# Square sums of latents, keys and channels: added over chunks on GpSimd and VectorE, then one TensorE product with a block of ones that sums and spreads

## The chip, the cores and the metric

One core of one Trainium2 chip runs the whole program. The metric is the device time in microseconds of one execution. The kernel is written directly on the engines: TensorE (PE), VectorE (DVE), ScalarE (ACT), GpSimd (POOL) and SyncE (SP) each have their own instruction list, and only semaphores order them against each other.

## The reference

Two transformer-like blocks of two layers each are run over 256 tokens (T) with a model width of 2048. The parts that matter are three norms inside each layer of the first block:

- Latents: z @ w_in gives a query latent of 512 and a key/value latent of 256 features. Each is divided per token by its root mean square, sqrt(mean(z²) + 1e-6), and multiplied by a gain.
- Keys: each of four heads has a key of 192 features, 128 of its own and 64 rotated ones that all heads share. Each is divided per token by the root mean square over the 192.
- Channels: the 512 channels of a causal 31-tap convolution go through a layer norm, so they need a mean and a mean of squares per token.

Everything is float32.

## The kernel before

Activations lie with features on the 128 partitions and tokens along the free axis, in chunks of 128 features; a tile of four chunks is 128 x 4 x 256. A norm therefore has to sum over partitions, which TensorE does by a product with ones, and the per-token result has to come back to every partition.

**Streams.** Weights come as slabs of 128 x 2048 float32 (1 MB), one DMA each on SyncE's queue into a ring of four (`raw`). ScalarE copies a slab to a rounded high part (`whi`, L1164, 1.92 us), VectorE subtracts to get the low part (`wlo`, L1630, 2.29 us), three slabs ahead of TensorE. TensorE multiplies each slab by the high and low parts of the activations H: 16 products of 512 columns (L642) and 16 of 256 (L653), about 5.5 us a slab. VectorE then takes the bank out and scales it (L1651, L1661).

**Order.** The first block's layer is a list of numbered slabs, by hand: zq 0 to 5, zkr 6, cfg 7 to 10, cfa 11 to 14, kv 15, qn 16, qr 17, ret 18 to 25, sc 26 to 37, rg 38 to 41, then wo. Each engine walks through the same numbers. For slab s it does its stream work and then the side work tied to s: TensorE in `within_first` (inside the slab) and `behind_first` (behind it), ScalarE in `beside_first`, VectorE in `before_first` and `after_first` (before and after its split). Side work on an engine stands in its program order, so whatever it waits for holds up the slab work behind it.

**The three norms before.** All three use the columns trick. The squares are the stationary operand and a single column of ones is streamed, which gives a sum per token on partitions (128 tokens at a time); ScalarE takes a root over a few columns, VectorE inverts them (`invert`, L1679), and `spread` (L767) brings them back by a product of the broadcast column with the identity.

- Latents: ScalarE squares into w4 and z[12:14] at slab 5; `lora_sums` (L758) runs within slab 7 and behind slab 7, 6 products of one column each time; root at 8 (L1280), invert at 8, spread of 4 behind 9, `lora_scaled` (L1782) at 9; `lora_low` at 11 hands the result to kv at slab 15.
- Keys: the rotated key is squared at 9 and the keys at 15 (ScalarE, L1266); `key_sums` (L776, L779) is called behind 16, between the units qn and qr, 10 products; then four transposes (L879); root (L1299) and `invert` at 16; `spread` of 8 behind 18; `keys_scaled` (L1812, L1816) at 18 reads the spread from PSUM. `query_turned` (L1825 to L1827) follows at 19, and `scores` (L840) behind slab 20 wait for it.
- Channels: VectorE computes the 31 taps of chunks 24 and 25 of z (L1774), GpSimd those of 26 and 27 (L529) out of products that ScalarE makes (L1381). `channel_sums` (L807) behind 36 adds the four chunks by four products with ones; VectorE centres them at 36 (L1902), ScalarE squares at 37 (L1266), `channel_squares` (L815) behind 38 takes 8 one-column products; root at 38 (L1324), invert, `spread` of 2 behind 39, scaling at 39 (L1909).

Each float32 product stands as two instructions in the trace (a count of x8 is four products). GpSimd is idle during slabs 0 to 12 and after its last tap (slab 28) until wo. Lengths that matter: `rstd` is 128 x 512, `tmp` 128 x 4 x 256, `sqacc` and `sqtmp` 128 x 256.

```python
def rooted(n=T, o=0):
    dve.wait_ge(S("root"), nth("root"))
    link(dve.reciprocal(rstd[:, o:o + n], rstd[:, o:o + n]))
def invert(columns):
    dve.wait_ge(S("root"), nth("root"))
    dve.reciprocal(inv_rms[:, 0:columns], inv_rms[:, 0:columns]).then_inc(S("inverted"), 1)
```

Of the kernel before, what the change touches and what calls it, by code (L numbers as in the profile page):

```python
# [27 lines left out]
P = 128  # L28
# [227 lines left out]
def _build(nc, d, out, ctx):  # L256
# [205 lines left out]
    def _(pool):  # L462
# [54 lines left out]
        for l in range(L):  # L517


            for c in POOL_CF:  # L520
# [3 lines left out]
                for s in range(1, 31):  # L524
# [6 lines left out]
                    done["tap"] += 1  # L531
            square_sum(slab_of(("wo", l)))
# [30 lines left out]
    def _(pe):  # L563
# [189 lines left out]
        def lora_sums(l, t):  # L753

            pe.wait_ge(S("lora_sq"), l + 1)
            for first, count, src in ((0, 4, w4[:, 0:4, :]), (2, 2, z[:, 12:14, :])):
                for c in range(count):
                    last = pe.matmul(pX[:, first + t:first + t + 1], src[:, c, t * P:(t + 1) * P], ones[:, 0:1],  # L758
                                     start=c == 0, stop=c == count - 1, skip_group_check=True)
            if t:  # L760
                last.then_inc(S("lora_sums"), 1)

        def spread(places):

            pe.wait_ge(S("inverted"), nth("spread"))
            for dst, c in places:
                last = pe.matmul(dst, inv_rms[:, c:c + 1].to_broadcast([P, P]), C("ident"),  # L767
                                 start=True, stop=True, skip_group_check=True)
            last.then_inc(S("spread"), 1)

        def key_sums(l):

            pe.wait_ge(S("key_sq"), l + 1)
            for t in range(2):
                tok = slice(t * P, (t + 1) * P)
                pe.matmul(pX[:, 4 * t:4 * t + 4], z[:, 6, tok], C("halves", 0, 1).to_broadcast([P, 4]), start=True,  # L776
                          stop=False, skip_group_check=True)
                for h in range(HEADS):
                    last = pe.matmul(pX[:, 4 * t + h:4 * t + h + 1], w4[:, h, tok], ones[:, 0:1], start=False,  # L779
                                     stop=True, skip_group_check=True)  # L780
            last.then_inc(S("key_sums"), 1)
# [20 lines left out]
        def channel_sums(l):  # L802

            pe.wait_ge(S("cf_taps"), 31 * len(DVE_CF) * (l + 1))
            pe.wait_ge(S("cf_pool"), 30 * len(POOL_CF) * (l + 1))
            for c in range(4):
                last = pe.matmul(pX[:, 0:T], ones[:], z[:, 24 + c, :], start=c == 0, stop=c == 3)  # L807
            last.then_inc(S("cf_sum"), 1)

        def channel_squares(l):  # L810

            pe.wait_ge(S("cf_sq"), l + 1)
            for t in range(2):
                for c in range(4):
                    last = pe.matmul(pX[:, t:t + 1], z[:, 16 + c, t * P:(t + 1) * P], ones[:, 0:1], start=c == 0,  # L815
                                     stop=c == 3, skip_group_check=True)
            last.then_inc(S("cf_sums"), 1)
# [147 lines left out]
        def within_first(l, s):  # L965

            if s == 7:
                if l == 0:
                    pe.wait_ge(S("const_in"), 16)
                lora_sums(l, 0)  # L970
# [10 lines left out]
        def behind_first(l, s):  # L981
# [10 lines left out]
            if s == 13:  # L992
                pe.wait_ge(S("turn_gains"), l + 1)
                pe.wait_ge(S("evac"), by["zkr", l].first + 1)
                turn_halves(vtok[:, 0:P], [small[:]], pO)
# [6 lines left out]
            if s == 18:  # L1002
                spread([((pX, pX, pO, pO)[h][:, (h % 2) * T + t * P:(h % 2) * T + (t + 1) * P], 4 * t + h)
# [1279 lines left out]
```

## Time and profile before

| what | value |
|---|---|
| device time, median of 3 runs | 3350.71 us (3349.78 to 3351.73) |
| the profiled execution's own time | 3352.41 us |
| its span, first to last instruction | 3350.2 us |
| mean granted TensorE clock | 0.998 |
| TensorE busy | 3327.6 us, 99% |
| VectorE, ScalarE, GpSimd busy | 78%, 46%, 26% |

Times in the views are microseconds from the span's start. A line such as `start length engine line operation out<-in shape xcount` merges neighbouring instructions of one kind; a bracket behind it is idle time of that engine before it and what ended it. A product's duration includes its way through the array, so products overlap: what a group costs TensorE is read from its start to the start of what comes next. Layer 0 of the first block runs its slabs 0 to 41 from about 11 to 284, layer 1 from about 1209 to 1475.

### The profile page before, as it was taken

The numbers are of one execution on the slowest core, as the hardware profiler recorded it, in microseconds if no ns is written. First come the engines' busy times: TensorE is split into PE (matmuls) and PEld (weight loads), VectorE is DVE, ScalarE is ACT, GpSimd is POOL, SyncE is SP. The second block draws the span as 40 slices with busy tenths as digits, with TensorE's granted clock in tenths as the row PEclk, the third lists the DMA queues.
The fourth block names the chain that finished last, engine by engine and source line by source line (L and its number), as shares of the span: only waits on it lengthen the run. The fifth ranks groups of instructions, "written<-read, shape, count | busy, mean of one in ns | idle before, by whom it ended". The sixth has DMA issues, their size and how long they took to land. (4 is left out here: it accounts for less than half of the span.)

```text
span 3350.2 us, 53769 instructions
## 1 busy us (share of the span) xinstructions
PE 3327.6 (99%) x20366; PEld 2929.1 (87%) x20366; DVE 2617.8 (78%) x3394; ACT 1531.6 (46%) x1642; POOL 864.2 (26%) x633
## 2 busy tenths in 40 slices
PE   9999999999999999999999999999999999999998
PEld 8989888888888989888888888888888888888897
DVE  8897788787786888887887787867867866678865
ACT  5644444343433556544443434335444444445443
POOL 0422432121122423414332121214432004150004
PEclk9999999999999999999999999999999999999999
DMA  6445555555555554455555555555544455544454
GB/s 241 148 163 176 189 188 189 178 202 177 206 174 189 203 182 165 151 176 187 190 188 178 198 180 199 180 190 200 193 164 153 167 173 189 180 164 151 167 185 151
DMA packets 90647, 605.21 MB, mean 181 GB/s; under 512 B 10192, under 2 KB 10352, under 8 KB 29296
## 3 DMA queue, kind: packets, MB, share of 16 engines
q1 hardware_dynamic: 89424, 599.83, 52.0%
q10 hardware_dynamic: 1056, 3.11, 0.2%
q8 instruction: 110, 1.80, 0.2%
q14 instruction: 57, 0.47, 0.0%
HBM read 600.80 MB, written 2.10 MB: 180 GB/s over the span
## 5 line engine op out<-in xcount | busy, mean ns | idle before, releaser
L642 PE MATMUL bank<-H,whi 128*128 128x512 f32 x6496 | 1574.3, 393 | 1.5 <-DVE z L1661 1.5
L1164 ACT ACTIVATE whi<-raw 128x2048 fp32r<-128x2048 f32 (+2 forms) x609 | 1093.6, 1796 | 1044.6 <-DMA raw<-in_slabs_down 259.8
L1630 DVE TENSOR_TENSOR wlo<-raw,whi 128x2048 fp32r<-128x2048 f32 (+2 forms) x609 | 1328.4, 2181 | 243.2 <-ACT whi L1164 233.1
L642 PEld LDWEIGHTS bank<-H,whi 128*128 128x128 f32 x6496 | 1188.7, 188 | 238.6 <-issue 5.9
L653 PEld LDWEIGHTS bank<-H,wlo 128*128 128x128 f32 x6624 | 849.1, 188 | 34.3
L653 PE MATMUL bank<-H,wlo 128*128 128x256 f32 x6624 | 871.1, 281 | 0.0
L511 POOL TENSOR_TENSOR sqtmp<-tmp 128x256 f32<-128x256 f32 x88 | 218.9, 2488 | 867.8 <-DVE tmp L2211 867.8
L642 PE MATMUL bank<-G,whi 128*128 128x512 f32 x1408 | 343.0, 391 | 0.0
L642 PEld LDWEIGHTS bank<-G,whi 128*128 128x128 f32 x1408 | 255.4, 188 | 48.0
L1564 ACT ACTIVATE G<-sqtmp 128x256 f32 (+1 forms) x88 | 36.8, 418 | 404.0 <-POOL sqtmp L511 404.0
L489 POOL TENSOR_TENSOR sqacc<-sqacc,sqtmp 128x256 f32<-128x256 f32 x119 | 199.4, 1676 | 9.4
L1651 DVE TENSOR_REDUCE tmp<-bank 128x256 f32<-128x512 f32 x216 | 149.0, 690 | 65.9 <-PE bank L653 65.4
L484 POOL TENSOR_TENSOR sqtmp<-x 128x256 f32<-128x256 f32 x119 | 133.7, 1123 | 238.5 <-DVE x L1705 182.5
L653 PEld LDWEIGHTS bank<-G,wlo 128*128 128x128 f32 x1408 | 184.3, 189 | 9.8
L529 POOL TENSOR_TENSOR z<-z,y 128x255 f32<-128x255 f32 (+14 forms) x120 | 121.1, 1009 | 269.9 <-ACT y L1381 254.2
L1704 DVE TENSOR_TENSOR x<-x,bank 128x256 f32 (+1 forms) x192 | 80.7, 420 | 138.8 <-PE bank L653 138.7
L653 PE MATMUL bank<-G,wlo 128*128 128x256 f32 x1408 | 186.8, 281 | 0.0
L1651 DVE TENSOR_REDUCE z<-bank 128x256 f32<-128x512 f32 x132 | 91.0, 690 | 103.1 <-PE bank L653 102.0
L484 POOL TENSOR_TENSOR sqacc<-x 128x256 f32<-128x256 f32 x8 | 16.3, 2031 | 589.0 <-DVE x L1705 547.1
L676 PE MATMUL bank<-whi,H 128*128 128x512 f32 x320 | 129.9, 406 | 0.0
L678 PE MATMUL bank<-whi,H 128*128 128x512 f32 x320 | 126.1, 394 | 0.0
L677 PE MATMUL bank<-wlo,H 128*128 128x512 f32 x320 | 126.0, 394 | 0.0
(390 smaller groups left out, 2881.4 us busy)
## 6 DMA issues: line engine op xcount, KB each, us to landing
raw<-in_slabs_up SPq DMA_DIRECT2D x176, 1024.0 KB, 4.8
raw<-in_slabs_down SPq DMA_DIRECT2D x128, 704.0 KB, 4.0
raw<-in_slabs_wo SPq DMA_DIRECT2D x32, 1024.0 KB, 4.8
raw<-in_slabs_pg SPq DMA_DIRECT2D x32, 1024.0 KB, 4.9
raw<-in_slabs_gates SPq DMA_DIRECT2D x32, 1024.0 KB, 4.9
raw<-in_slabs_wout SPq DMA_DIRECT2D x32, 1024.0 KB, 4.8
raw<-in_slabs_sc SPq DMA_DIRECT2D x24, 1024.0 KB, 4.8
raw<-in_slabs_fox SPq DMA_DIRECT2D x24, 1024.0 KB, 4.9
```

The source lines that it names most:

```text
L484: pool.tensor_tensor((sqtmp if c else sqacc)[:], x[:, c, :], x[:, c, :], ALU.mult).then_inc(S("pool_sq"), 1)
L489: ins = pool.tensor_tensor(sqacc[:], sqacc[:], sqtmp[:], ALU.add)
L511: pool.tensor_tensor(act_f[:], tmp[:, 3, :], tmp[:, 2, :], ALU.mult).then_inc(S("act_f32"), 1)
L529: pool.tensor_tensor(o[:, s:T], o[:, s:T], product[:, done["tap"] % TAP_RING, s:T], ALU.add).then_inc(S("cf_pool"), 1)
L642: pe.matmul(b[0:r.m, :], whi[:, n % RAW, w], r.src[:, k, :], start=at == 0, stop=False)
L653: last = pe.matmul(b[0:r.m, 0:T], wlo[:, n % RAW, w], r.src[:, k, 0:T], start=False, stop=at == r.kt - 1)
L676: pe.matmul(b[:], high, whi[:, n % RAW, w], start=k == 0, stop=False)
L677: pe.matmul(b[:], high, wlo[:, n % RAW, w], start=False, stop=False)
L678: last = pe.matmul(b[:], low, whi[:, n % RAW, w], start=False, stop=k == DC - 1)
L1164: act.activation(whi[:, n % RAW, 0:w], raw[:, n % RAW, 0:w], ACT.Copy).then_inc(S("hi_ready"), 1)
L1630: dve.tensor_tensor(wlo[:, n % RAW, 0:w], raw[:, n % RAW, 0:w], whi[:, n % RAW, 0:w].bitcast(F32), ALU.subtract).then_inc(S("lo_ready"), 1)
L1651: return dve.tensor_reduce(dst, b[0:m, :].rearrange("p (h t) -> p t h", h=2), AX, ALU.add)
```

## The change

All three norms give up the columns. The squares are first added over their chunks, so that one product per norm with the full 128 x 128 block of ones as stationary operand and the added squares (256 columns) streamed gives the sum already on every partition. Root and reciprocal then run over full width instead of a few columns, and the spread products go.

- Latents: GpSimd waits for the squares and makes three adds (512, 256 and 256 columns wide); `lora_sums` is two products behind slab 7; ScalarE's root covers 2 x 256 columns, VectorE's reciprocal (`rooted`) 512 columns at slab 9.
- Keys: ScalarE halves the shared square (one more activation); VectorE adds it to all four heads' squares (`keys_added`, 1024 columns) at slab 15 behind `key_rope`; `key_sums` waits for that add and is four products into pX and pO; the root covers 2 x 512 columns; VectorE's reciprocal covers 1024 (`keys_inverse`) at slab 16.
- Channels: GpSimd adds the four convolution chunks (three adds) and, after ScalarE's squares, the four squares (two adds, 512 and 256 wide); `channel_sums` and `channel_squares` are one product each; the reciprocal covers 256 columns at slab 39.

```diff
@@ gpsimd, start of each layer @@
+            pool.wait_ge(S("lora_sq"), l + 1)
+            pool.tensor_tensor(w4[:, 0:2, :], w4[:, 0:2, :], w4[:, 2:4, :], ALU.add).then_inc(S("lora_added"), 1)
+            pool.tensor_tensor(z[:, 12, :], z[:, 12, :], z[:, 13, :], ALU.add).then_inc(S("lora_added"), 1)
+            pool.wait_ge(S("lora_added"), 3 * l + 2)
+            pool.tensor_tensor(w4[:, 0, :], w4[:, 0, :], w4[:, 1, :], ALU.add).then_inc(S("lora_added"), 1)
@@ gpsimd, behind the taps @@
+            pool.wait_ge(S("cf_pool"), done["tap"])
+            pool.tensor_tensor(sqtmp[:], z[:, 26, :], z[:, 27, :], ALU.add).then_inc(S("cf_added"), 1)
+            pool.wait_ge(S("cf_taps"), 31 * len(DVE_CF) * (l + 1))
+            pool.tensor_tensor(sqacc[:], z[:, 24, :], z[:, 25, :], ALU.add).then_inc(S("cf_added"), 1)
+            pool.wait_ge(S("cf_added"), 3 * l + 2)
+            pool.tensor_tensor(sqacc[:], sqacc[:], sqtmp[:], ALU.add).then_inc(S("cf_added"), 1)
+            pool.wait_ge(S("cf_sq"), l + 1)
+            pool.tensor_tensor(z[:, 16:18, :], z[:, 16:18, :], z[:, 18:20, :], ALU.add).then_inc(S("cf_sq_added"), 1)
+            pool.wait_ge(S("cf_sq_added"), 2 * l + 1)
+            pool.tensor_tensor(z[:, 16, :], z[:, 16, :], z[:, 17, :], ALU.add).then_inc(S("cf_sq_added"), 1)
@@ tensor @@
-        def lora_sums(l, t):
...
-        def spread(places):
...
+        def lora_sums(l):
+            pe.wait_ge(S("lora_added"), 3 * (l + 1))
+            pe.matmul(pX[:, 0:T], ones[:], w4[:, 0, :], start=True, stop=True, skip_group_check=True)
+            pe.matmul(pX[:, T:2 * T], ones[:], z[:, 12, :], start=True, stop=True,
+                      skip_group_check=True).then_inc(S("lora_sums"), 1)
@@ key_sums @@
-            pe.wait_ge(S("key_sq"), l + 1)
...
+            pe.wait_ge(S("key_added"), l + 1)
+            for h in range(HEADS):
+                last = pe.matmul((pX, pX, pO, pO)[h][:, (h % 2) * T:(h % 2) * T + T], ones[:], w4[:, h, :], start=True,
+                                 stop=True, skip_group_check=True)
@@ channel_sums, channel_squares @@
+            pe.wait_ge(S("cf_added"), 3 * (l + 1))
+            pe.matmul(pX[:, 0:T], ones[:], sqacc[:], start=True, stop=True).then_inc(S("cf_sum"), 1)
...
+            pe.wait_ge(S("cf_sq_added"), 2 * (l + 1))
+            pe.wait_ge(S("cf_centred"), 4 * (l + 1))
+            pe.matmul(pX[:, 0:T], ones[:], z[:, 16, :], start=True, stop=True).then_inc(S("cf_sums"), 1)
@@ within_first, behind_first @@
-                lora_sums(l, 0)
...
-                lora_sums(l, 1)
-            if s == 9:
-                spread([(pX[:, c * P:(c + 1) * P], c) for c in range(4)])
+                lora_sums(l)
...
-            if s == 18:
-                spread([((pX, pX, pO, pO)[h][:, (h % 2) * T + t * P:(h % 2) * T + (t + 1) * P], 4 * t + h)
-                        for h in range(HEADS) for t in range(2)])
...
-            if s == 39:
-                spread([(pX[:, c * P:(c + 1) * P], c) for c in range(2)])
@@ scalar @@
+                for g, width in ((0, 512), (1, 256)):
+                    last = act.activation(rstd[:, g * T:g * T + T], pX[:, g * T:g * T + T], ACT.Sqrt, scale=1.0 / width,
+                                          bias=eps[:])
...
+                link(act.activation(z[:, 6, :], small[:], ACT.Square))
+                act.activation(z[:, 6, :], z[:, 6, :], ACT.Copy, scale=0.5).then_inc(S("rope_key_sq"), 1)
...
+                for p, px in enumerate((pX, pO)):
+                    last = act.activation(tmp[:, 2 * p:2 * p + 2, :].rearrange("p a t -> p (a t)"), px[:], ACT.Sqrt,
+                                          scale=1.0 / 192, bias=eps[:])
...
+                act.activation(rstd[:, 0:T], pX[:, 0:T], ACT.Sqrt, scale=1.0 / 512, bias=eps[:]).then_inc(S("root"), 1)
@@ vector @@
+        def rooted(n=2 * T):
+            dve.wait_ge(S("root"), nth("root"))
+            link(dve.reciprocal(rstd[:, 0:n], rstd[:, 0:n]))
...
         def lora_scaled(l):
-            dve.wait_ge(S("spread"), nth("spread"))
+            rooted()
...
+        def keys_added(l):
+            dve.wait_ge(S("key_sq"), l + 1)
+            rope = z[:, 6:7, :].to_broadcast([P, HEADS, T])
+            dve.tensor_tensor(w4[:], w4[:], rope, ALU.add).then_inc(S("key_added"), 1)
+        def keys_inverse():
+            dve.wait_ge(S("root"), nth("root"))
+            link(dve.reciprocal(tmp[:], tmp[:]))
...
             if s == 15:
                 key_rope(l)
-            if s == 8:
-                invert(4)
+                keys_added(l)
...
             if s == 16:
-                invert(8)
+                keys_inverse()
...
             if s == 39:
-                dve.wait_ge(S("spread"), nth("spread"))
+                rooted(T)
```

`lora_scaled`, `keys_scaled` and the channels' scaling now read the inverse from SBUF (`rstd`, `tmp`) instead of PSUM.

## Rows read from the trace of the kernel before

**Rows 1.** The page: busy us (share of the span) and instructions per engine.

```profile
PE 3327.6 (99%) x20366; PEld 2929.1 (87%) x20366; DVE 2617.8 (78%) x3394; ACT 1531.6 (46%) x1642; POOL 864.2 (26%) x633
```

**Rows 2.** Waits of TensorE: us in total, times, longest us.

```profile
PE pS L840 <- DVE z L1827: 1.5, 2, 0.9
```

**Rows 3.** Timeline of TensorE, layer 1, 1253 to 1267: start us, us, what.

```profile
1253.41 0.95 PE L758 MATMUL pX<-ones,w 128*128 128x1 f32 x8
...
1254.66 3.88 PE L642 MATMUL bank<-H,whi 128*128 128x512 f32 x16
...
1265.81 1.05 PE L767 MATMUL pX<-cst,inv_rms 128*128 128x128 f32 x8
1266.62 0.70 PE L642 MATMUL bank<-H,whi 128*128 128x512 f32 x2
```

**Rows 4.** Timeline of TensorE, layer 1, 1305.9 to 1308.6.

```profile
1306.17 0.28 PE L776 MATMUL pX<-cst,z 128*128 128x4 f32 x2
...
1308.32 0.53 PE L879 MATMUL pS<-cst,z 128*128 128x128 f32 x3
```

**Rows 5.** Timeline of TensorE, layer 1, 1443 to 1466.

```profile
1443.48 1.89 PE L807 MATMUL pX<-z,ones 128*128 128x256 f32 x8
1445.02 4.02 PE L642 MATMUL bank<-H,whi 128*128 128x512 f32 x16
...
1456.31 1.84 PE L815 MATMUL pX<-ones,z 128*128 128x1 f32 x16
1458.01 3.92 PE L642 MATMUL bank<-H,whi 128*128 128x512 f32 x16
```

**Rows 6.** Timeline of TensorE, layer 1, 1288 to 1293.5.

```profile
1288.87 0.59 PE L799 MATMUL pO<-small,vtok 128*128 128x256 f32 x2
1289.12 4.02 PE L642 MATMUL bank<-H,whi 128*128 128x512 f32 x16
```

**Rows 7.** Groups of VectorE by shape: busy us, mean ns of one | idle before.

```profile
L1675 DVE RECIPROCAL rms<-rms 128x256 f32<-128x256 f32 x8 | 14.0, 1748 | 7.7 <-ACT rms L1219 7.7
...
L2130 DVE TENSOR_TENSOR y<-y 128x1024 f32<-128x1024 f32 x3 | 3.7, 1226 | 1.6 <-ACT y L1533 1.5
...
L1679 DVE RECIPROCAL inv_rms<-inv_rms 128x8 f32<-128x8 f32 x2 | 0.4, 194 | 0.0
```

**Rows 8.** Timelines of VectorE, layer 1: two operations' ends.

```profile
1307.85 0.52 DVE L1804 TENSOR_TENSOR small<-small,tmp 128x256 f32<-128x256 f32 x1
...
1334.72 0.69 DVE L1827 TENSOR_TENSOR z<-z,tmp 128x512 f32<-128x512 f32 x1
```

**Rows 9.** Stretches: length, busy us (count) per engine, granted clock, DMA share, GB/s.

```profile
75.00:117.75 42.75, 42.75 (x287) 39.51 (x286) 41.47 (x60) 27.43 (x34) 12.23 (x11) 0.99 0.52 179
1264.20:1283.50 19.30, 19.30 (x121) 17.34 (x120) 14.65 (x18) 8.90 (x8) 0.00 (x0) 1.00 0.48 171
1312.84:1335.40 22.56, 21.69 (x183) 21.39 (x182) 17.25 (x22) 13.88 (x22) 14.41 (x16) 1.00 0.42 141
3342.00:3344.00 2.00, 0.00 (x0) 0.00 (x0) 1.96 (x2) 0.00 (x0) 0.00 (x0) 0.58 0.00 0
```

**Rows 10.** Timeline of ScalarE, layer 1: the root of the key sums.

```profile
1311.39 0.27 ACT L1299 ACTIVATE inv_rms<-pX,eps 128x8 f32<-128x8 f32 x1
```

**Rows 11.** Timeline of TensorE, layer 0, 113.9 to 114.1.

```profile
114.02 0.28 PE L776 MATMUL pX<-cst,z 128*128 128x4 f32 x2
```

**Rows 12.** Timeline of GpSimd, layer 1: two taps, the first beside a VectorE split.

```profile
1293.58 2.58 POOL L529 TENSOR_TENSOR z<-z,y 128x254 f32<-128x254 f32 x1 [0.17 <-POOL z L529]
...
1297.39 0.72 POOL L529 TENSOR_TENSOR z<-z,y 128x252 f32<-128x252 f32 x1 [0.17 <-POOL z L529]
```

**Rows 13.** Timeline of ScalarE, layer 1: squares of the channels.

```profile
1451.60 1.06 ACT L1266 ACTIVATE z<-z 128x1024 f32<-128x1024 f32 x1 [1.13 <-DVE z L1902]
```

**Rows 14.** Timeline of VectorE, layer 1: the split behind those squares, and slab 39.

```profile
1454.89 2.29 DVE L1630 TENSOR_TENSOR wlo<-raw,whi 128x2048 fp32r<-128x2048 f32 x1
...
1463.85 0.69 DVE L1651 TENSOR_REDUCE z<-bank 128x256 f32<-128x512 f32 x1 [3.01 <-PE bank L653]
```

More of the change, by code:

```diff
@@ L1278, in beside_first @@
                 act.wait_ge(S("lora_sums"), l + 1)
-                for g, width in ((0, 512), (2, 256)):
-                    last = act.activation(inv_rms[:, g:g + 2], pX[:, g:g + 2], ACT.Sqrt, scale=1.0 / width, bias=eps[:])
+                for g, width in ((0, 512), (1, 256)):
+                    last = act.activation(rstd[:, g * T:g * T + T], pX[:, g * T:g * T + T], ACT.Sqrt, scale=1.0 / width,
+                                          bias=eps[:])
                 last.then_inc(S("root"), 1)
@@ L1290, in beside_first @@
             if s == 9:
-                squares(z[:, 6, :], small[:], "rope_key_sq", (S("evac"), by["zkr", l].first + 1))
+                act.wait_ge(S("evac"), by["zkr", l].first + 1)
+                link(act.activation(z[:, 6, :], small[:], ACT.Square))
+                act.activation(z[:, 6, :], z[:, 6, :], ACT.Copy, scale=0.5).then_inc(S("rope_key_sq"), 1)
             if s == 15:
@@ L1298, in beside_first @@
                 act.wait_ge(S("key_sums"), l + 1)
-                act.activation(inv_rms[:], pX[:, 0:8], ACT.Sqrt, scale=1.0 / 192, bias=eps[:]).then_inc(S("root"), 1)
+                for p, px in enumerate((pX, pO)):
+                    last = act.activation(tmp[:, 2 * p:2 * p + 2, :].rearrange("p a t -> p (a t)"), px[:], ACT.Sqrt,
+                                          scale=1.0 / 192, bias=eps[:])
+                last.then_inc(S("root"), 1)
                 act.wait_ge(S("unit_taken"), 4 * l + 4)
@@ L1675, in inverse @@
             link(dve.reciprocal(rms[:], rms[:]))
-        def invert(columns):
-            dve.wait_ge(S("root"), nth("root"))
-            dve.reciprocal(inv_rms[:, 0:columns], inv_rms[:, 0:columns]).then_inc(S("inverted"), 1)
         def x_lo(g, l, lo=0, hi=DC):
@@ L1804, in key_rope @@
             link(dve.tensor_tensor(small2[:], small2[:], tmp[:, 1, :], ALU.add), "key_rope")
+        def keys_added(l):
[5 more added lines that the diff above has]
+            link(dve.reciprocal(tmp[:], tmp[:]))
         def keys_scaled(l):
[L1808 removed]
             dve.wait_ge(S("g_qk"), l + 1)
[L1810 to L1813 removed]
+            for p in range(2):
+                kk, inverse = z[:, 8 + 2 * p:10 + 2 * p, :], tmp[:, 2 * p:2 * p + 2, :]
+                dve.scalar_tensor_tensor(kk, kk, g_qk[:, l:l + 1], inverse, ALU.mult, ALU.mult)
                 for e in range(2):
                     half = slice(64 * e, 64 * e + 64)
[L1816 removed]
+                    ins = dve.tensor_tensor(z[half, 6 + p, :], small2[half, :], inverse[half, e, :], ALU.mult)
             ins.then_inc(S("keys_scaled"), 1)
```

50 lines of the change are left out of this document (4 added, 46 removed).

## The prediction

> **What bounds the kernel now.** I read the page first: TensorE is busy 99% of the span [rows 1]. So I went to TensorE's waits, to see whether anything is left there to take. One wait of the changed part stands there, before the scores behind slab 20, on the last step of VectorE's query rotation: 1.5 us in two times [rows 2]. Two consequences. Every microsecond of TensorE work removed is a microsecond gained, as long as TensorE then finds its next operand ready; and at one place per layer VectorE is already as late as TensorE, so work added to VectorE ahead of it is paid in full. The rest is therefore a reading of timelines: what each replaced product costs TensorE, and where the engines that take the work over stand when TensorE comes by.
>
> **What TensorE loses and gains, per layer.** Costs go from a group's start to the next work's start.
> - Latent sums: 1.25 us behind slab 7 (1253.41 to 1254.66) and as much within it; spread behind 9: 0.81 [rows 3].
> - Key sums: 2.15 [rows 4]. The spread of eight behind 18: at twice the 0.81 for four, 1.62.
> - Channel sums 1.54, squares 1.70 [rows 5]; the spread of two, at half the 0.81, 0.40.
>
> That is 10.7 us. Added are eight float32 products of 256 columns. One alone takes 0.25 (1288.87 to 1289.12) [rows 6], each further one in a row 0.385 (1.54 over four, rows of the channel sums). Latents 0.63, keys 1.40, channels 0.25 twice: 2.53. TensorE saves 8.2 per layer, 16.4 us in all, 0.5% of the time. Of this, 2.7 is its lead when it reaches the key sums (2.50 + 0.81 - 0.63).
>
> **What VectorE gets.** The inverses grow from a few columns to 512, 1024 and 256. A reciprocal of 256 columns takes 1.748 us and one of 8 takes 0.194 [rows 7], so 6.27 ns a column: 3.35 for 512 and 6.56 for 1024. That is five times what an add of 1024 takes, 1.226 (same rows), which is the price of `keys_added`. Per layer 3.35 + 1.23 + 6.56 + 1.75 = 12.9 us go on VectorE; the column reciprocals that come off cost 0.2 each. Reading the inverse from SBUF in place of PSUM I cost at nothing: the reads are as wide as before.
>
> **The key sums, layer 1.** The new wait is for `keys_added`, which stands behind the split and `key_rope` of slab 15. In the trace `key_rope` ends at 1307.85 + 0.52 = 1308.4 [rows 8], yet key sums start at 1306.2 [rows 4]: they did not need it before. Now they do. Does `key_rope` move? Ahead of it lies the reciprocal of 512, 3.35. In the stretch from the outlet of slab 9 to the end of slab 11's side work VectorE is busy 14.65 of 19.30 [rows 9]; the 4.65 of idle are waits for slabs, and those come 1.9 to 2.7 earlier now. 4.65 against 3.35: `key_rope` ends 1.3 earlier, at 1307.1, the add at 1308.3. TensorE comes at 1306.2 - 2.7 = 1303.5 and stands 4.8 us. Behind that wait are the transposes, unit qr and the whole stream.
>
> Then the chain to the scores. Key sums, 1.4, end at 1309.7. Before, ScalarE's root ended 3.34 after them (1308.32 to 1311.66) [rows 4, 10]; two roots of 512 in place of one of 8 columns add 0.9. Root at 1314.0, the reciprocal of 1024 ends at 1320.6. Before, the step behind this reciprocal began at 1312.84, and from there to the end of the query rotation (1334.72 + 0.69 = 1335.4 [rows 8]) VectorE was busy 17.25 of 22.56 [rows 9]; the idle 5.3 was waiting for slabs that are now ready early. So the rotation ends near 1338.1. TensorE, with no spread to do, is there some 4 us before and stands a second time. The scores start **2.7 us later** than before.
>
> **Layer 0.** Here the setup of the angles fills VectorE: 41.47 busy of the 42.75 up to the end of `key_rope` at 117.75 [rows 9], with no wait in it, so the 3.35 is hidden only by the 1.2 that it waited for slabs 8 and 9. `key_rope` ends at 119.8, the add at 121.0; key sums began at 114.02 [rows 11] and would come at 111.3: near 10 us of standing (part of it may show earlier, at unit kv, which needs the bank of slab 14 taken out). Root 121.0 + 1.4 + 4.2 = 126.7, reciprocal to 133.3, 17.1 of work behind it: scores at 150.4 where they were at 144.4, **6.0 us later**. Up to the scores the change costs 8.7 us over both layers, the savings counted.
>
> **Latents on GpSimd.** The squares end one slab ahead of the sums and GpSimd is idle. Three adds take 2.9 us at 0.72 a tap of about 256 columns, and one can be held while a split runs on VectorE: such a tap took 2.58 [rows 12]. In layer 1 that is in time; in layer 0 it may be 2 us late, but TensorE then only stands less at the key sums. Cost nothing; if that cover is gone, up to 2.
>
> **Channels.** Sums: GpSimd's taps end long before, VectorE's at slab 34; three adds, each at most 2.6, are ready before slab 36 ends. Saved 1.29. Squares: ScalarE's end at 1451.60 + 1.06 = 1452.66 [rows 13]. GpSimd then adds 512 columns, about 1.5, and would start the second add at 1454.5, beside VectorE's next multiply and its split from 1454.89 to 1457.18 [rows 14]. From the held tap I take it that this add waits: ready at 1457.9. TensorE comes at 1456.31 - 1.29 = 1455.0 and stands 2.8. Bounds: 0.3, if the add slips in, and 2.9. The reciprocal of 256 at slab 39 is covered by the 3.01 us that VectorE idles there (same rows). Per layer 3.64 - 0.50 - 2.8 = 0.3 saved, 0.6 in all; with the add in time 5.6.
>
> The Trainium skill, page "GPSIMD Engine Reference", section 1 (Specifications), says that GpSimd's SBUF interface is shared with VectorE and that VectorE instructions with two SBUF inputs contend for it. By it the second add is held; without it the sum would be 5 us lower. The taps of 2.58 and 0.72 agree.
>
> **The clock.** The granted clock is full through layer 1; it fell once at the very end, right behind the last products (mean 0.58 over 3342 to 3344) [rows 9]. No row shows what a stand of 3 to 5 us inside the stream does. If the clock is at half behind the scores' wait for some 3 us, 1.5 us is lost per layer, and as much at the key sums, partly hidden by the second wait. Between 0 and 8 us in all I take 3.
>
> The Trainium skill, page "TensorE: Matmul & The Clock Gate", section "What's actually happening", has the throttled state as the default that activity releases. By it each of the four waits ends at half clock; a kernel that kept every wait short would lose nothing.
>
> **The sum.** 8.7 - 0.6 + 3 = +11.1 us on the profiled execution's 3352.4 (the span of 3350.2 and 2.2 around it). The median of the runs is 3350.7, 1.7 below it, so the forecast is **3362 us**. By itself it runs from 8.7 - 5.6 + 0 = +3 to 8.7 + 8 = +17: 3354 to 3368.
>
> **Rivals.**
> - *The wide reciprocals cost like an add.* Place: VectorE between slabs 9 and 16. The forecast hangs on 6.27 ns a column. If a wide one ran at the add's 1.2 ns, the 1024 would take 1.2 and the 512 0.7: in layer 0 the first lateness shrinks by 2.6 and the scores come 2 later instead of 6, bounded by TensorE; in layer 1 they come 2 earlier. With the channels -0.6 to -5.6: about -3, **3348**. It decides for "not slower" from a reciprocal of 1024 under about 2.5 us. Against it: eight reciprocals of 256 all took 1.75. For it: no row wider than 256. 0.1.
> - *No wait appears*: VectorE reaches the key add before TensorE does, which needs it 5 us (layer 1) and 10 us (layer 0) earlier. Then the products' saving stands alone: -16.4, **3334**. The views speak against it. 0.07.
> - *The clock stays full and GpSimd's add is in time*: +3, **3354**. 0.18.
> - *The lateness spreads*: while VectorE is 6 us behind, its splits come late too, and TensorE stands again behind the scores, or the clock falls longer at all six waits: twice the cost up to the scores, +20, **3371**. For it: VectorE is near full there. Against it: the splits run three slabs ahead. 0.12.
> - Forecast: 0.53.
>
> **Range and chances.** 3346 to 3372 leaves out the second rival, the upper part of the fourth and a little of the first. A measurement of this kernel tells about 0.2%, 6.7 us, from no change. Slower by more: the forecast nearly whole (0.50) and the spread of lateness (0.12). Within: the third rival (0.18), most of the first (0.07), the forecast's lower end (0.03): 0.28. Faster: the second (0.07) and a little of the first (0.03): 0.10.
>
> **What would show it.** TensorE's waits should hold a new line for the key sums on VectorE's add, some 5 us in layer 1 and up to 10 in layer 0, a larger one at the scores' line on the query rotation, 4 us each, and one for the channel squares on GpSimd, 2 to 3 each. The groups of VectorE should show a reciprocal of 1024 at 6.6 and one of 512 at 3.35. TensorE's busy time should fall by about 16. I am wrong if the reciprocal is far shorter, if key sums do not wait, or if the waits are there and the time still falls.

## The result, and the profile after

The changed kernel takes **3376.48 us** (median of 6 runs, 3375.54 to 3377.22) beside 3351.28 for the kernel before on the same chip: ratio **1.0073**, 95% interval 1.0063 to 1.0083. It is 25 us slower; the forecast was 11 slower, with 3372 as the top of the range. The profiled execution has a span of 3374.5 us. What follows compares it with the one before (span 3350.2). Two executions of later runs fell into a much slower state at a lower clock (3619.69 us of `chan_only`, 5623.22 of a kernel before beside `before_thin`) and count in no ratio.

The page's busy line (us, share, instructions) answers to [rows 1]:

```profile
PE 3324.6 (99%) x20206; PEld 2921.9 (87%) x20206; DVE 2652.9 (79%) x3396; ACT 1535.0 (45%) x1646; POOL 872.0 (26%) x649
```

TensorE has 3.0 us less busy time, not 16: of the 16.4 us that the products save, most is given back by work at a lower clock (below), and the span grew by 24.3 us of standing and slow work. Its waits (us in total, times, longest), which answer to [rows 2]:

```profile
PE pS L834 <- DVE z L1823: 12.4, 2, 6.2
PE pX L779 <- DVE w L1797: 10.8, 2, 5.4
...
PE bank L760 <- issue: 2.5, 1, 2.5
PE bank L760 <- DVE z L2150: 1.5, 1, 1.5
```

The wait for the scores went from 1.5 us to 12.4, the forecast's new wait for the key add (L1797) is there with 5.4 us in each layer, and 4.0 us are stood at unit kv of layer 0. None is for GpSimd's channel squares.

TensorE's timeline of layer 1 (start us, us, what), which answers to [rows 4]; the sums, the transposes behind them, and the first scores:

```profile
1323.12 2.07 PE L779 MATMUL pX<-w,ones 128*128 128x256 f32 x4 [5.40 <-DVE w L1797]
...
1326.69 1.06 PE L873 MATMUL pS<-cst,z 128*128 128x128 f32 x4
...
1358.06 0.58 PE L834 MATMUL pS<-z 128*128 128x128 f32 x1 [6.17 <-DVE z L1823]
```

The key sums last from 1323.12 to 1326.69, 3.57 us, where the forecast had 1.4 and the run `fill` below shows 1.83 at full clock. VectorE's side of the same chain: the key add, the reciprocal, the last step of the rotation:

```profile
1321.84 1.22 DVE L1797 TENSOR_TENSOR w<-w,z 128x1024 f32<-128x1024 f32 x1
...
1331.79 6.55 DVE L1802 RECIPROCAL tmp<-tmp 128x1024 f32<-128x1024 f32 x1 [4.41 <-ACT tmp L1288]
...
1357.31 0.69 DVE L1823 TENSOR_TENSOR z<-z,tmp 128x512 f32<-128x512 f32 x1
```

VectorE's groups by shape (busy us, mean ns of one | idle before):

```profile
L1802 DVE RECIPROCAL tmp<-tmp 128x1024 f32<-128x1024 f32 x2 | 13.1, 6553 | 8.4 <-ACT tmp L1288 8.4
...
L1812 DVE TENSOR_TENSOR z<-small,tmp 64x256 f32<-64x256 f32 x8 | 7.1, 882 | 0.1
...
L1661 DVE RECIPROCAL rstd<-rstd 128x512 f32<-128x512 f32 x2 | 6.7, 3350 | 0.0
...
L1809 DVE SCALAR_TENSOR_TENSOR z<-z,g_qk,tmp 128x512 f32<-128x512 f32 x4 | 4.6, 1148 | 0.0
...
L1797 DVE TENSOR_TENSOR w<-w,z 128x1024 f32<-128x1024 f32 x2 | 2.4, 1224 | 0.1
```

The reciprocals of 1024 (6.55) and 512 (3.35) and the add (1.22) are as forecast to 0.01 us. The scaled keys (L1809, L1812) are not what they were. These are two of their four groups before the change, which read the inverse from PSUM:

```profile
L1816 DVE TENSOR_TENSOR z<-small,pX 64x256 f32<-64x256 f32 x4 | 1.7, 415 | 0.0
...
L1812 DVE SCALAR_TENSOR_TENSOR z<-z,g_qk,pO 128x512 f32<-128x512 f32 x2 | 1.5, 748 | 0.0
```

742 to 748 ns became 1148, and 415 became 882: (1148 - 745) x 2 + (882 - 415) x 4 = 2.7 us more per layer, on the path to the scores.

In the next view the granted clock (1.00 is full, 0.50 the lower of its two levels) is the first number behind the five engines' busy times. Stretches behind the key sums' and the scores' starts, layers 0 and 1, which answer to [rows 9]:

```profile
122.40:126.40 4.00, 3.87 (x10) 3.01 (x11) 3.89 (x6) 0.00 (x0) 0.00 (x0) 0.50 0.00 0
157.00:169.00 12.00, 11.91 (x64) 10.28 (x64) 7.07 (x16) 4.90 (x10) 2.78 (x3) 0.69 0.01 1
1323.00:1327.00 4.00, 3.88 (x10) 3.06 (x11) 3.90 (x6) 0.00 (x0) 0.00 (x0) 0.50 0.00 0
1358.00:1370.00 12.00, 11.94 (x63) 10.45 (x63) 6.83 (x16) 4.82 (x10) 2.77 (x3) 0.67 0.01 1
```

The clock is at its lower level, half, for the key sums and the transposes behind them, and for 7 to 8 of the 12 us behind the scores: (1 - 0.69) x 12 = 3.7 us and (1 - 0.67) x 12 = 4.0 us of work lost there. Accordingly the second scores come 11.1 and 11.3 us after the first in place of 7.8.

The kernel before was not at full clock throughout either. In layer 0, right behind its key sums and with no wait of TensorE, the same view shows:

```profile
117.00:119.00 2.00, 2.00 (x11) 2.00 (x10) 1.90 (x5) 1.79 (x3) 0.00 (x0) 0.50 0.65 274
```

Over 117 to 121 the mean was 0.61, 1.6 us of work lost; behind the key sums of layer 1 it stayed at 1.00 (1309 to 1311).

The channels, TensorE's timeline, answering to [rows 5]:

```profile
1470.08 0.60 PE L805 MATMUL pX<-sqacc,ones 128*128 128x256 f32 x2
1470.33 4.01 PE L657 MATMUL bank<-H,whi 128*128 128x512 f32 x16
...
1481.72 0.70 PE L811 MATMUL pX<-z,ones 128*128 128x256 f32 x2
1482.07 0.59 PE L657 MATMUL bank<-H,whi 128*128 128x512 f32 x1
```

Sums cost 0.25 us and squares 0.35, where they were 1.54 and 1.70 with a spread behind.

**Where the time went.** Starts of TensorE's work, after minus before: layer 0's scores +12.6, its second scores +15.9, layer 1's start +14.1; layer 1's scores +22.6, its second scores +26.1, the last product +24.2. So the scores come 12.6 us later in layer 0 and 8.5 in layer 1, another 3.3 and 3.5 us are lost behind them, and 1.8 and 1.9 come back later in the layer, at the channels.

### The profile page after: what moved, and what is told of

The parts are those of the page before. It is cut to its first block and busy times, and to the rows that moved or that the text cites. A ratio compares the mean times of both kernels' runs of the same rounds, so it can differ in the third digit from the quotient of the medians.

```text
span 3374.5 us, 53471 instructions
## 1 busy us (share of the span) xinstructions
PE 3324.6 (99%) x20206; PEld 2921.9 (87%) x20206; DVE 2652.9 (79%) x3396; ACT 1535.0 (45%) x1646; POOL 872.0 (26%) x649
## 5 line engine op out<-in xcount | busy, mean ns | idle before, releaser
L489 POOL TENSOR_TENSOR sqacc<-sqacc,sqtmp 128x256 f32<-128x256 f32 x119 | 183.2, 1540 | 9.4
L484 POOL TENSOR_TENSOR sqacc<-x 128x256 f32<-128x256 f32 x8 | 15.9, 1993 | 468.2 <-DVE x L1692 427.0
```

Source lines behind the costliest of these rows:

```text
L484: pool.tensor_tensor((sqtmp if c else sqacc)[:], x[:, c, :], x[:, c, :], ALU.mult).then_inc(S("pool_sq"), 1)
L489: ins = pool.tensor_tensor(sqacc[:], sqacc[:], sqtmp[:], ALU.add)
```

## Experiments

Every group of runs had the kernel before beside it (medians 3351.7 to 3352.8); differences are of medians against that one. The changed kernel itself was timed in one group only, 25.2 us over (21 to 28 by its interval). "Off" for an edit of the changed kernel means 25.2 less what the edited kernel is over its own before, and the ranges given with it take the 25.2 as it stands.

### One part of the change at a time

`chan_only` has only the hunks of the channels, `lat_only` only those of the latents, `keys_only` only those of the keys:

```diff
 chan_only: GpSimd's five channel adds, channel_sums, channel_squares, rooted(T) at slab 39
 lat_only:  GpSimd's three latent adds, lora_sums(l), two roots into rstd, rooted(2 * T)
 keys_only: keys_added, key_sums with four products, two roots into tmp, keys_inverse, keys_scaled
```

> Only the channels' part of the change on the kernel before. Theory (the loss lies up to the scores, the channels' part gains): TensorE saves 1.3 us at the sums and some 1.4 at the squares per layer, GpSimd's adds are in time, as the trace of the changed kernel shows no wait there: 5 to 6 us off in all, near 3346 us. The prediction's own term (the second add held by VectorE's split): 0.6 us off, near 3351.

Measured: 3347.88 us, **3.8 off**, ratio 0.9988 (0.9978 to 0.9997). The interval is 1 to 7 us off. The prediction's 0.6 lies just outside it, and TensorE has no wait for GpSimd's channel adds in this trace, so the term for a held add fails; the theory's 5 to 6 can't be told from 3.8.

> Only the latents' part on the kernel before. Theory (what VectorE gets ahead of the keys is paid where VectorE sets the pace): TensorE saves 2.7 us per layer, the reciprocal of 512 puts 3.35 us on VectorE; in layer 1 idle time covers it and about 1 us is gained, in layer 0 the scores come some 2 us later: between 3349 and 3356 us, and with a half clock behind longer stands at the upper end. Rival (the latents' reciprocal is what makes the keys late): 8 us or more slower, 3359 or above. Rival (it is covered): 5.4 us off, 3346.

Measured: 3353.17 us, 1.5 more, ratio 1.0003 (0.9994 to 1.0012), which can't be told from no change. The two layers differ as expected: the second scores of layer 0 come 7.4 us later than before, and from there to layer 1's it is 2.5 us less. The 7.4 overstates layer 0: the profiled execution, 3358.07 us, is the slowest of the eleven. At 38 us it stood 3.0 in place of 1.5, with the clock at 0.58 and 0.56 in the 4 us behind, some 3.3 us together. The rest of what layer 0 pays with stands in TensorE's waits, the ones at unit kv (L750) above all:

```profile
PE bank L750 <- DVE z L2154: 3.1, 1, 3.1
...
PE pS L842 <- DVE z L1826: 1.6, 2, 1.1
...
PE bank L750 <- issue: 0.8, 1, 0.8
```

> Only the keys' part on the kernel before. Theory (the chain key add, key sums, root, reciprocal of 1024, scaled keys, rotation is the cost, and TensorE's clock falls behind both of its stands): the scores come 6 to 7 us later per layer with some 4 us of half clock behind: 3370 to 3377 us, nearly the whole loss. Rival (the loss needs the latents' reciprocal in front of it): under 3363 us. With both other parts measured alone, the three differences should add up to the 25 us of the whole change if nothing is shared between them.

Measured: 3376.27 us, **24.6 more**, ratio 1.0074 (1.0061 to 1.0088). The keys' part alone makes the whole loss; the latents' reciprocal in front is not needed for it. TensorE's waits:

```profile
PE pS L836 <- DVE z L1834: 11.2, 2, 6.2
PE pX L775 <- DVE w L1808: 9.2, 2, 5.3
```

The sum is -3.8 + 1.5 + 24.6 = 22.3 beside 25.2 for the whole. The 3 us between are within what these runs can tell (the interval of `keys_only` alone is 20 to 29).

### The inverse read from PSUM

```diff
-            link(dve.reciprocal(tmp[:], tmp[:]))
+            for p, px in enumerate((pX, pO)):
+                last = dve.reciprocal(px[:], tmp[:, 2 * p:2 * p + 2, :].rearrange("p a t -> p (a t)"))
+            link(last)
...
-                kk, inverse = z[:, 8 + 2 * p:10 + 2 * p, :], tmp[:, 2 * p:2 * p + 2, :]
+                kk, inverse = z[:, 8 + 2 * p:10 + 2 * p, :], (pX, pO)[p][:].rearrange("p (a t) -> p a t", a=2)
```

> The changed kernel, with the wide reciprocal of the keys written to the two PSUM banks that the sums were in, so that the scaled keys read the inverse from PSUM as they did before. Theory (the read from SBUF is what doubled the scaled keys from 3.0 to 5.9 us): they take 3.0 again, the chain to the scores is 2.9 us shorter per layer, 5.8 us off the changed kernel: near 3370.5 us. Rival (their length has another cause): 5.9 us stays, 3376 us.

Measured: 3369.47 us, 17.7 over before where the changed kernel is 25.2 over: **7.5 off**; ratio 1.0047 (1.003 to 1.0064), that is 10 to 21 over and 4 to 15 off. Two of the four groups of the scaled keys, back at their old durations:

```profile
L1814 DVE TENSOR_TENSOR z<-small,pO 64x256 f32<-64x256 f32 x4 | 1.7, 414 | 0.0
...
L1811 DVE SCALAR_TENSOR_TENSOR z<-z,g_qk,pX 128x512 f32<-128x512 f32 x2 | 1.5, 736 | 0.0
```

The rotation ended 2.7 us earlier in layer 0 and, that gain carried, 5.7 in layer 1. So the read is a cost of its own: the multiplies are the same, the inverse lies in the other memory, and beside that only the reciprocal is split into two of 512.

### GpSimd's taps nearly gone

Each of the 60 adds that make up GpSimd's taps in a layer works on 8 columns, which leaves most of them out of the computation; once on the changed kernel, once on the one before.

```diff
-                    pool.tensor_tensor(o[:, s:T], o[:, s:T], product[:, done["tap"] % TAP_RING, s:T],
+                    pool.tensor_tensor(o[:, s:s + 8], o[:, s:s + 8], product[:, done["tap"] % TAP_RING, s:s + 8],
```

> The changed kernel with GpSimd's taps of the channel filters on 8 columns each in place of 226 to 255, which leaves most of these taps out of the computation; it asks whether GpSimd's work beside it is what makes the scaled keys slow. Theory (two SBUF sources on VectorE while GpSimd runs on SBUF): with GpSimd nearly idle the scaled keys take about 3 us per layer in place of 5.9, and the time falls by up to 7 us from 3376.5. Rival (two SBUF sources are slow of themselves): 5.9 us stays.

Measured: 3350.67 us, ratio to before 0.9991 (0.9981 to 1.0001). The scaled keys, with the inverse still in SBUF, are quick:

```profile
L1812 DVE TENSOR_TENSOR z<-small,tmp 64x256 f32<-64x256 f32 x8 | 3.4, 422 | 0.1
...
L1809 DVE SCALAR_TENSOR_TENSOR z<-z,g_qk,tmp 128x512 f32<-128x512 f32 x4 | 3.0, 750 | 0.0
```

So it isn't SBUF that is slow, but two SBUF sources beside a working GpSimd. The time fell by 26 to 27 us, though, where the scaled keys explain 5.4 directly and 7.5 by the run above. TensorE's two waits shrank too:

```profile
PE pS L834 <- DVE z L1823: 4.5, 2, 2.4
PE pX L779 <- DVE w L1797: 3.4, 2, 2.1
```

Other VectorE instructions with two SBUF sources gained as well: in layer 1, from the rotation product of the keys (behind slab 13) to the end of `key_rope`, VectorE needs 17.5 us (1289.77 to 1307.23) in place of 21.65 (1300.15 to 1321.80). With the key add earlier the stands are short, and less work falls to the half clock. ScalarE, which makes the products for GpSimd's taps, waits less for GpSimd too, but that isn't the way the gain came: in this stretch VectorE of the changed kernel waits for nothing, and behind it only for the root.

> The kernel before with GpSimd's taps on 8 columns each, which leaves most of these taps out of the computation, as in the run of the changed kernel that ended at 3350.7 us; it gives that run its own before. Theory (before, TensorE sets the pace and VectorE has room, so a faster VectorE brings nearly nothing; the change's cost lies in VectorE working beside GpSimd and in the clock): 3347 to 3350 us, so that without GpSimd's work the change costs 0 to 3 us in place of 25. Rival (GpSimd's work costs the kernel before as much as the changed one): 3326 us, and the change costs 25 us all the same.

Measured: 3350.71 us, ratio 0.9993 (0.9983 to 1.0003). Without GpSimd's taps beside it **the change costs nothing that these runs can tell**: 2.2 and 1.8 us under the kernel before, each within 3.4, where with the taps it costs 25. It gains nothing either: the 16.4 us of products saved are still lost to the stands and the clock. The kernel before hardly cares; its TensorE is busy 99% and waited 1.5 us in all for the scores.

### Stands filled with products

```diff
+        def filled(n):
+            for _ in range(n):
+                pe.matmul(pX[:, 0:T], ones[:], ones[:, 0:1].to_broadcast([P, T]), start=True, stop=True, skip_group_check=True)
...
         def key_sums(l):
+            filled(12)
             pe.wait_ge(S("key_added"), l + 1)
...
+                if s == 20:
+                    pe.wait_ge(S("keys_scaled"), l + 1)
+                    filled(14)
                 pe.wait_ge(S("query_turned"), l + 1)
```

> The changed kernel with 12 float32 products of ones by ones ahead of the wait for the key sums and 14 ahead of the wait for the first scores, 4.6 and 5.4 us at full clock, which nothing reads; nothing else is touched. Theory (a good part of the loss is TensorE's half clock behind its stands): the clock stays full, the key sums take 1.4 us in place of 3.6 and the stretch behind the scores some 4 us less: 8 to 13 us off, 3363 to 3368 us, though the engine gets more work. Rival (the stands are the loss and the clock hardly counts): 3374 to 3378 us, or more where the products outlast the waits.

Measured: 3367.22 us, **9.7 off** the changed kernel's distance to before; ratio 1.0049 (1.0032 to 1.0065), 3 to 14 off. The stretches that answer to the four above:

```profile
122.00:126.00 4.00, 4.00 (x27) 3.75 (x28) 3.89 (x5) 1.51 (x3) 0.00 (x0) 1.00 0.00 0
154.00:166.00 12.00, 11.88 (x78) 9.87 (x77) 9.93 (x23) 5.27 (x12) 2.77 (x3) 1.00 0.25 81
1317.00:1321.00 4.00, 3.97 (x27) 3.72 (x28) 3.90 (x5) 1.49 (x3) 0.00 (x0) 1.00 0.02 4
1349.00:1361.00 12.00, 11.87 (x78) 9.86 (x77) 9.94 (x23) 5.24 (x12) 2.77 (x3) 1.00 0.25 82
```

Clock 1.00 in all four, where it was 0.50 and 0.67 to 0.69. The key sums take 1.83 us in place of 3.57 and the second scores follow 7.8 us after the first. TensorE does more, and the kernel is faster: the half clock costs about 10 us. The roots, too, end 4.31 us behind the key sums in both layers, where in the changed kernel they ended 4.67 and 5.07 behind them, with the transposes at half clock in between. The Trainium skill, page "TensorE: Matmul & The Clock Gate", section "What's actually happening", says that activity releases the throttle; by it the filler should hold the clock, and the stretches agree.

### Both, and the inverse's length

`psum_fill` joins the two edits, with 7 products ahead of the scores in place of 14.

> The changed kernel with both: the inverse of the keys written to PSUM, 12 products that nothing reads ahead of the wait for the key sums and 7 ahead of the first scores. Theory (the two costs, 7.0 and 9.3 us when each is taken away alone, are separate): 16 us off, 3360 us, which is what the forecast would be with the clock at nothing and the read at nothing. Rival (with the shorter stand the clock would have cost less, so they overlap): 3364 us.

Measured: 3363.44 us, ratio 1.0033 (1.0022 to 1.0044), **14.6 off** (10 to 18) where the two alone add to 17.2. That lies between the theory's 16 and the 12.5 or so of the rival, and can't tell them apart; whether the two costs overlap stays open. Part of the difference is the filler's own: in this trace key sums and scores start 1.2, 0.9, 0.1 and 0.9 us after what they wait for.

`narrow` takes the reciprocal of the keys over 8 columns, so the inverse is left out of the computation:

```diff
-            link(dve.reciprocal(tmp[:], tmp[:]))
+            link(dve.reciprocal(tmp[:, 0, 0:8], tmp[:, 0, 0:8]))
```

> The changed kernel with the keys' reciprocal over 8 columns in place of 1024; the rest of the keys is scaled by the root itself, which leaves the inverse out of the computation. Theory (the reciprocal lies whole on the chain, and the clock is lost behind the scores' stand): 6.4 us less on the chain per layer, the scores' stand of 6.2 us is nearly gone and with it about 4 us of half clock: 17 to 21 us off, 3355 to 3359 us. Rival (the clock falls anyway): 12.7 off, 3364 us. Rival (the wide reciprocal is covered): under 4 off.

Measured: 3365.17 us, ratio 1.0045 (1.0028 to 1.0061): 11.8 off (5 to 16), near the first rival's 12.7 and short of the theory's 17 to 21. TensorE's timeline, first and second scores of layer 1:

```profile
1346.09 2.70 PE L834 MATMUL pS<-z 128*128 128x128 f32 x8 [2.62 <-DVE z L1823]
...
1356.95 0.82 PE L834 MATMUL pS<-z 128*128 128x128 f32 x4
```

The theory was wrong on the clock in layer 1: a stand of 2.6 us was left, and the second scores still came 10.9 us after the first. In layer 0, with 1.05 us left, it was 7.8. The reciprocal is about half of the loss; the rest stays without it.

### The wait alone

`add_only` is the kernel before with `keys_added`, the halved square that it needs, and its wait, and nothing else of the change: column sums (8 products in place of 10), narrow inverse, spread.

```diff
-            pe.wait_ge(S("key_sq"), l + 1)
+            pe.wait_ge(S("key_added"), l + 1)
...
+        def keys_added(l):
+            dve.wait_ge(S("key_sq"), l + 1)
+            rope = z[:, 6:7, :].to_broadcast([P, HEADS, T])
+            dve.tensor_tensor(w4[:], w4[:], rope, ALU.add).then_inc(S("key_added"), 1)
```

> The kernel before with one part of the keys' change: VectorE adds the rope half of the squares to all heads ahead of the key sums, which stay column products (8 in place of 10); narrow inverse and spread as before. Theory (the new wait alone is a real cost, the wide reciprocal adds to it): TensorE stands some 5 us at the key sums in layer 0 and 3 in layer 1, the clock falls behind each, part of it comes back from the idle time of VectorE behind: 5 to 10 us slower than before, 3357 to 3362 us. Rival (the wait is only a shift, the scores wait for VectorE as before): within 2 us of before.

Measured: 3367.06 us, **14.2 more**, ratio 1.0039 (1.0024 to 1.0055), 8 to 18 more: the median is above the theory's 5 to 10, the interval reaches into it, and the rival's 2 is excluded. By the medians more than half of the keys' loss comes from letting TensorE wait at this one place. It stood 5.1 us in layer 0 and 3.3 in layer 1, and its scores are 6.4 and 13.2 us late. Layer 1, key sums and scores:

```profile
1315.85 3.57 PE L777 MATMUL pX<-ones,w 128*128 128x1 f32 x16 [3.33 <-DVE w L1810]
...
1348.62 0.71 PE L838 MATMUL pS<-z 128*128 128x128 f32 x3 [0.48 <-DVE z L1833]
```

The 16 small instructions of the key sums take 3.57 us: the clock is at half again. It was 0.50 for 8 us behind each of the two stands and 0.87 and 0.85 in the 4 us after (117.86 to 129.86 and 1315.85 to 1327.85), some 4.5 us of work lost per layer. By estimate from these rows, the two stands (8.4) and the clock (9.1, less the 1.6 that the kernel before lost at this place) make 16, of which two products fewer per layer and shorter waits at the scores take a little off: the 14.2 is the stand and the slow clock behind it, and nothing absorbed it.

VectorE had 5.0 us of idle time between the key sums and the scores of layer 0 before, which the forecast spent to absorb lateness. Now it has more, not less. Three of its waits in that stretch, from its timeline (idle time in brackets, and what ended it); with two shorter ones they make 11.2 us:

```profile
125.49 0.20 DVE L1679 RECIPROCAL inv_rms<-inv_rms 128x8 f32<-128x8 f32 x1 [3.37 <-ACT inv_rms L1299]
127.83 0.69 DVE L2170 COPY z<-bank 128x512 f32<-128x512 f32 x1 [2.13 <-PE bank L749]
...
144.48 1.61 DVE L1774 SCALAR_TENSOR_TENSOR z<-z,cols 128x236 f32<-128x236 f32 x2 [4.17 <-PE bank L653]
```

The first is the root behind the later sums; in the others VectorE waits for slabs (`PE bank`) of a TensorE that stood for VectorE and then ran at half clock. Both engines are late together.

### Versions that could beat both

`chan_lath`: the channels' part, and GpSimd's adds for the latents with four column sums, narrow inverse and spread. `chan_lat1`: the same in layer 0, the latents' full new way in layer 1.

```diff
 chan_lath
+            for first, src in ((0, w4[:, 0, :]), (2, z[:, 12, :])):
+                for t in range(2):
+                    last = pe.matmul(pX[:, first + t:first + t + 1], src[:, t * P:(t + 1) * P], ones[:, 0:1],
+                                     start=True, stop=True, skip_group_check=True)
 chan_lat1
+            if l:
+                rooted(2 * T)
+            else:
+                dve.wait_ge(S("spread"), nth("spread"))
```

> The channels' part, and of the latents' part only GpSimd's adds: the sums stay column products (4 in place of 12) with a reciprocal of 4 columns and the spread; the keys stay as before. Theory (TensorE's work is gained where VectorE gets nothing for it): 5 to 6 us from the channels and 1.7 us per layer at the latents, 8 to 9 in all: near 3342 us. Rival (VectorE's query rotation sets the scores in both layers, so what the latents save is only stood there): as with the channels alone, near 3346 us.

Measured: 3347.41 us, 4.3 off; ratio 0.9987 (0.9978 to 0.9996). That is `chan_only` to half a microsecond, the rival's figure, but not by the rival's mechanism: TensorE waits 1.2 us on VectorE at the scores, where `chan_only` waits 1.8, so the saving is not stood there. Against `chan_only`, from layer 0's scores to layer 1's the trace is 2.0 us shorter; layer 0 lost 1.9, counted from the end of the stand near 38 us, which was 3.6 long here with the clock at 0.50 behind it. This profiled execution, 3350.99 us, is itself 3.6 above the median of its kernel, so where the saving goes in a usual execution isn't shown.

> The channels' part in both layers; of the latents' part GpSimd's adds in both, but the wide sums, root and reciprocal of 512 in layer 1 alone (layer 0 keeps column sums, 4 in place of 12, and the spread); the keys as before. Theory (the latents' part costs only where the setup fills VectorE, in layer 0): in the run of the latents alone layer 0 lost and layer 1 gained about 2.5 us; the channels alone stood at 3347.9, so near 3345 us. Rival (layer 1's gain is stood at the scores too): 3347 to 3348 us.

Measured: 3349.82 us, 3.0 off; ratio 0.9988 (0.9979 to 0.9997). No better either. In the trace layer 1 is 2.2 us shorter from second scores to second scores than with the channels alone, but layer 0 lost 3.2, with these waits in it:

```profile
PE pX L786 <- DVE inv_rms L1689: 2.3, 1, 2.3
PE bank L657 <- DVE z L1671: 2.1, 1, 2.1
```

The first is the spread of the latents on VectorE's narrow inverse; the second stands at 38 us and changes from profile to profile, from nothing to 4.1 us. The channels' part alone beats the kernel before by 0.12% (0.03 to 0.22) and the changed one by some 0.85%, and is what I would keep; `chan_lath` and `chan_lat1` can't be told from it.

## Why the prediction was wrong

Right: the direction, the place (VectorE's chain up to the scores), all three reciprocals and the add, the new stand at the key sums with its part at unit kv, the latents' small net, layer 0 the worse of the two. Against layer 1's own start, TensorE reached the key sums at 1303.6 (forecast 1303.5) and the key add ended at 1309.0 (1308.3). Wrong were the size, by 14 us, and the signs that TensorE's busy time would fall by 16 (it fell by 3.0) and that the scores would wait some 4 us (6.2). The steps:

1. **"Reading the inverse from SBUF in place of PSUM I cost at nothing: the reads are as wide as before."** It cost 2.7 us per layer directly and 7.5 us of the total (4 to 15). I looked at the width and not at what runs beside: GpSimd's taps, in the same stretch. The Trainium skill, page "GPSIMD Engine Reference", section 1, names VectorE instructions with two SBUF inputs as those that contend; moving the inverse from PSUM to SBUF turns the scaled keys from one SBUF input into two. By it they slow down here, and `psum_inv` (736 and 414 ns) and `pool_thin` (750 and 422) agree. I had drawn on the page for GpSimd's adds and didn't turn it on VectorE.

2. **The clock, "between 0 and 8 us in all I take 3".** Filling the stands brought 9.7 (3 to 14). The term was mis-sized twice: half clock lasts 7 to 8 us behind the scores, not 3, and the key sums with it are no hidden work but a link of the chain: 3.6 us, twice, instead of 1.4 (1.83 at full clock, so the price of the products was 0.4 low as well). The prediction's reading that the clock fell once, at the very end, also missed layer 0, where it was at 0.50 over 117 to 119.

3. **"the idle 5.3 was waiting for slabs that are now ready early".** The idle time did go: between the add and the end of the rotation VectorE waits only for the root. But the stretch behind the reciprocal took 19.7 us in both layers (137.36 to 157.03 and 1338.34 to 1358.00), not 17.1 and 17.5, which is step 1 again. (The rows give 1320.6 + 17.25 = 1337.9 for the end of the rotation, not 1338.1; that changes nothing.) And `add_only` shows that VectorE's idle time makes good nothing that TensorE loses: waits of 5.1 and 3.3 us cost 14.2, the half clock included.

4. **The channel squares, "From the held tap I take it that this add waits".** It didn't: the split came later than the add, and where the two engines did meet it was VectorE that lost time (a step of 256 columns, L2175, took 1.26 us beside the first add, where the kernel before has 0.35). GpSimd's adds in layer 1, and the VectorE split that I had put beside the second:

```profile
1479.35 1.49 POOL L544 TENSOR_TENSOR z<-z 128x512 f32<-128x512 f32 x1 [29.17 <-ACT z L1251]
1480.92 0.75 POOL L546 TENSOR_TENSOR z<-z 128x256 f32<-128x256 f32 x1
```

```profile
1482.84 2.28 DVE L1621 TENSOR_TENSOR wlo<-raw,whi 128x2048 fp32r<-128x2048 f32 x1
```

The add ended at 1481.67, just before TensorE came (1481.72), and the split began 1.2 us later. The gain is 3.8 us over both layers (`chan_only`), not 0.6.

As a sum over the runs: forecast 8.7 + 3 - 0.6 = 11. With what the runs measured in place of its terms: 8.7, 7.5 for the read, 9.7 for the clock, less 2.6 (17.2 against the 14.6 of both together), -3.8 for the channels: 19.5. That leaves 5.7 of the 25.2. The filler outlasting its waits hides some 3 of that in `psum_fill` (1.2 + 0.9 + 0.1 + 0.9), and the intervals of the single runs are wider than the rest.

The trace of the changed kernel closes it more finely. Over both layers, against the forecast and up to the scores:

- the key add ends 1.5 us later than forecast in layer 0 and 0.7 in layer 1: 2.2, and no run shows the cause;
- the key sums take 3.6 in place of 1.4: 4.3, of which 3.5 is the clock;
- the roots end 4.67 and 5.07 us behind the sums in place of 4.24: 1.3, of which 1.1 is the clock, by `fill`'s 4.31;
- the reciprocal is as forecast;
- the stretch behind it is 19.7 in place of 17.1 and 17.5: 4.7.

That is 12.5 on top of the 8.7, and the scores are indeed 12.6 + 8.5 = 21.1 us late. Behind them half clock adds 6.8, and 3.7 comes back later in the layers: 24.2, with 24.3 in the span. So in this trace the clock's term is 11.4 where 3 was forecast, and the read's 4.7 where nothing was.

The rival "the lateness spreads, or the clock falls longer" (3371) was the nearest one and had 0.12. Its second half came true: the clock was at half for much longer. Its first did not, as TensorE has no new wait on VectorE's splits behind the scores. That it also priced the cost up to the scores at about twice the forecast's, and that this was 21.1 in place of 8.7, is partly luck: the read from SBUF, which it doesn't name, is in that figure.

Not tried: GpSimd's taps moved to another stretch of the layer in the changed kernel. Their products come through a ring of four that ScalarE fills, so by the program a later start would hold ScalarE; no run shows at what price.

## What to carry to other kernels

Spreading a sum over all partitions before its inverse trades TensorE's cheap tiny products for a full-width reciprocal on VectorE (6.55 us for 1024 columns, where an add takes 1.22); do that only where VectorE is idle and nobody waits, as at the channels. When an operand moves from PSUM to SBUF, ask what GpSimd does in that stretch, even if shapes stay. And price a new wait of TensorE with what follows it, the stand and the slow clock behind it; idle time of another engine makes neither good.

## What I had not expected of the hardware

- VectorE's multiply of 128x512 from two SBUF sources took 0.75 us with GpSimd nearly idle and 1.15 beside its full taps; one of 64x256 0.42 and 0.88. With one source in PSUM it was 0.74 to 0.75 and 0.41 to 0.42, GpSimd working (the kernel before, `psum_inv`) or not (`before_thin`).
- At the key sums and the scores the granted clock did not fall behind stands of up to 1.3 us and fell behind all of 2.1 us and more. Elsewhere no length decides: behind the 2.5 us stand at unit kv it fell in the changed kernel (0.50 over 104 to 106), `narrow` and `pool_thin`, and stayed full in `fill`, `psum_inv` and `psum_fill` with the same stand. In the kernel before it fell to 0.50 behind the key sums of layer 0 with no stand at all.
- Work that nobody reads, put into TensorE's stands, made the kernel 9.7 us faster: the clock stayed at 1.00.
